# Attention in a one-core transformer block: the next head's high and low parts made in thirds on ScalarE and VectorE instead of whole on ScalarE and GpSimd

## The reference, cut to what matters

```python
def block_attention(q, k, v):          # q, k: 96 wide; v: 64 wide; 8 heads
    scale = dk ** -0.5
    qb = q.reshape(B, nb, Q_BLOCK, H, dk).transpose(1, 0, 2, 3, 4)
    def one_block(qblk):
        s = jnp.einsum('bqhd,bkhd->bhqk', qblk, k).astype(jnp.float32) * scale
        p = jax.nn.softmax(s, axis=-1).astype(v.dtype)
        return jnp.einsum('bhqk,bkhd->bqhd', p, v)
```

## Time and profile before

| what | value |
|---|---|
| three runs | 3381.17, 3385.09, 3386.98 us; median 3385.09 |
| the profiled execution's own time | 3376.51 us |
| its span, first to last instruction | 3374.7 us |
| mean granted TensorE clock | 0.944 |
| TensorE busy | 3056.5 us, 91% of the span |
| VectorE busy | 1946.7 us, 58% |
| ScalarE busy | 1373.7 us, 41% |
| GpSimd busy | 648.9 us, 19% |

### The profile page before, as it was taken

One profiled execution on the slowest core, in us unless ns is written; L12 is line 12 of the kernel. 1 busy time (PEld: TensorE's weight loads), 2 busy tenths in 40 slices (PEclk: granted clock), 3 DMA queues, 4 the chain that ended last, 5 costly groups with the idle time before them and its releaser, 6 DMA issues. The chain is left out here.

```text
span 3374.7 us, 43955 instructions
## 1 busy us (share of the span) xinstructions
PE 3056.5 (91%) x14693; PEld 2172.2 (64%) x14693; DVE 1946.7 (58%) x2632; ACT 1373.7 (41%) x2061; POOL 648.9 (19%) x459
## 2 busy tenths in 40 slices
PE   6799999999887699999999999799399999999992
PEld 1355555555587455655665565687399899989992
DVE  1133333333476578777777776445767666767663
ACT  0133333333222556656665665211244444444442
POOL 0011111111254233232233222221001010101011
PEclk9899999999877899999999999899599999999996
DMA  8512111111221201101110100433467576767666
GB/s 318 155 63 69 64 62 62 65 66 57 86 95 55 50 4 32 33 7 29 33 26 10 32 5 5 171 131 112 139 203 219 184 221 201 220 189 224 201 179 237
DMA packets 254709, 363.74 MB, mean 108 GB/s; under 512 B 36436, under 2 KB 170583, under 8 KB 252888
## 3 DMA queue, kind: packets, MB, share of 16 engines
q1 hardware_dynamic: 245336, 327.97, 30.4%
q0 software_dynamic: 9216, 33.56, 4.4%
HBM read 279.65 MB, written 81.83 MB: 107 GB/s over the span
## 5 line engine op out<-in xcount | busy, mean ns | idle before, releaser
L467 PE MATMUL bank<-w_in_sb,h_T 128*128 128x512 f32 (+1 forms) x1440 | 609.3, 578 | 2.1 <-DVE h_T L616 2.1
L1648 PE MATMUL ebank<-gathered_T,w_gate_up 128*128 128x256 f32 x4608 | 561.6, 284 | 22.8 <-issue 13.8
L1648 PEld LDWEIGHTS ebank<-gathered_T,w_gate_up 128*128 128x128 f32 x4608 | 557.3, 191 | 26.5 <-issue 17.6
L1077 PE MATMUL abank<-scores,head_v 128*128 128x512 f32 x1152 | 547.1, 603 | 2.2 <-ACT scores L1115 2.2
L1040 PE MATMUL abank<-head_qT,head_kT 96*128 96x512 f32 x1728 | 505.4, 437 | 24.2 <-POOL head_qT L1019 24.2
L467 PEld LDWEIGHTS bank<-w_in_sb,h_T 128*128 128x128 f32 x1440 | 270.1, 191 | 299.0 <-issue 298.8
L1040 PEld LDWEIGHTS abank<-head_qT,head_kT 96*128 96x128 f32 x1728 | 327.9, 190 | 171.9 <-issue 95.8
L1103 ACT ACTIVATE scores<-abank 128x512 f32<-128x512 f32 x576 | 314.5, 608 | 77.5 <-PE abank L1040 71.7
L1077 PEld LDWEIGHTS abank<-scores,head_v 128*128 128x128 f32 x1152 | 218.4, 194 | 181.4 <-issue 163.8
L1026 POOL TENSOR_TENSOR scores<-scores,max_for_pool 128x1536 f32<-128x1536 f32 x64 | 221.0, 3474 | 571.9 <-ACT max_for_pool L1109 571.9
L1115 ACT ACTIVATE scores<-scores 128x1536 f32<-128x1536 f32 x192 | 287.4, 1498 | 40.0 <-DVE scores L1157 35.6
(11 more groups left out here) (258 smaller groups left out, 3465.2 us busy)
## 6 DMA issues: line engine op xcount, KB each, us to landing
w_gate_up_whole<-in_w_exp_gate SPq DMA_DIRECT2D x48, 1024.0 KB, 5.6
w_gate_up_whole<-in_w_exp_up SPq DMA_DIRECT2D x48, 1024.0 KB, 9.0
w_down_whole<-in_w_exp_down SPq DMA_DIRECT2D x192, 256.0 KB, 4.8
ada_w<-in_w_ada SPq DMA_DIRECT2D x12, 2048.0 KB, 12.6
scratch_ret<-ret_rows SPq DMA_DIRECT2D x72, 256.0 KB, 2.6
x_tile<-in_x_all SPq DMA_DIRECT2D x18, 512.0 KB
w_in_sb<-in_w_in SPq DMA_DIRECT2D x4, 2048.0 KB, 19.0
chunk_qk<-scratch_ret SPq DMA_DIRECT2D x16, 512.0 KB
```

Source lines behind the costliest of these rows:

```text
L467: m = pe.matmul(banks[bank][:, 0:n], hT[u][:, k, :], w_in[:, k, lo:lo + n], start=(k == 0), stop=(k == KD - 1))
L1077: m = pe.matmul(banks[5 + j % 2][:, :], v1[u][:, kt, :], sc[j % 2][:, kt, :], start=(kt == 0), stop=(kt == T - 1))
L1648: x = pe.matmul(banks[f % 3][:, j * CAP:(j + 1) * CAP], w_gu[c][:, wp, j, k, o:o + P], xsT[:, xp, k, :], start=(k == 0 and n == 0), stop=( ...
```

## The change

- A turn's split is now a third of the columns (768; of the queries 768, 768 and 512). Turns `j` 0, 1, 2 split the odd head of the pair, turns 4, 5, 6 the even head of the next.
- ScalarE makes the rounded copies of the third where it made the whole ones, behind the last copy of scores and ahead of the copy of the maxima.
- The subtractions move from GpSimd to VectorE, and stand behind the shift of groups 0 and 1 and ahead of the output.
- The first head's split is in thirds on ScalarE and VectorE too.
- Keys and queries count into one semaphore per parity, values into another. ScalarE waits for keys and queries alone. TensorE waits for the first head's values and for the ones column only behind the first block's scores.
- `modulation`'s semaphores are cleared and freed behind its block, and an empty block (a barrier) follows.

```diff
@@ -116,6 +116,21 @@
     return parts, whole
 
 
+@contextmanager
+def stage_semaphores(nc):
+
+    taken = []
+
+    def sem(name):
+        taken.append(nc.alloc_semaphore(name=name))
+        return taken[-1]
+
+    yield sem
+    nc.clear_and_free_semaphores(taken)
+    with nc.Block():
+        pass
+
+
 def mid(ap, n):
 
     p, a = ap.shape
@@ -144,12 +159,9 @@
 
 def modulation(nc, ins, perm, scratch, weights, w_loaded):
 
-    with ExitStack() as ctx:
+    with stage_semaphores(nc) as sem, ExitStack() as ctx:
         def sb(name, shape, dt=F32):
             return ctx.enter_context(nc.sbuf_tensor(name, shape, dt))
-
-        def sem(name):
-            return ctx.enter_context(nc.semaphore(name))
 
         NCH = 12
         CW = 6 * D // NCH
@@ -964,7 +976,7 @@
         o_sb = sb("out_T", [64, QB])
         ms = sb("max_for_pool", [P, QB])
         banks = [ctx.enter_context(nc.psum_tensor(f"abank{b}", [P, 512], F32)) for b in range(8)]
-        kv_loaded = ParitySignal(nc, ctx, "head_kv_loaded", 4)
+        kq_loaded, v_loaded = ParitySignal(nc, ctx, "head_kq_loaded", 3), ParitySignal(nc, ctx, "head_v_loaded")
         ones_set = ctx.enter_context(nc.semaphore("ones_set"))
         assert nc.sbuf_base <= perm["mix_at"], (nc.sbuf_base, perm["mix_at"])
         block = ctx.enter_context(nc.Block())
@@ -977,21 +989,28 @@
             for j in range(2 * NB):
                 turn(H // 2 - 1, j, BLOCKS - 2 * NB + j, j < 2 * NB - 1)
 
+        THIRD = TOK // 3
+
+        def thirds(u, n):
+
+            c = slice(n * THIRD, (n + 1) * THIRD)
+            return (kT[u], k_whole[u], c), (qT[u], q_whole[u], slice(c.start, min(c.stop, SEQ)))
+
         def split_next(split, pair, j):
 
-            if j == 1:
-                split(pair * 2 + 1, 1)
-            if j == 5 and not (isinstance(pair, int) and pair == H // 2 - 1):
-                split(pair * 2 + 2, 0)
+            if j < 3:
+                split(pair * 2 + 1, 1, j)
+            if 4 <= j < 7 and not (isinstance(pair, int) and pair == H // 2 - 1):
+                split(pair * 2 + 2, 0, j - 4)
 
         @block.sync
         def _(sp):
             def load(head, u):
-                for dst, src in ((k_whole[u][0:NOPE, 1, :], scratch["kT_heads"][bass.ds(head, 1), :, :].rearrange("o d n -> (o d) n")),
-                                 (k_whole[u][NOPE:DQ, 1, :], scratch["krT"]),
-                                 (q_whole[u][:, 1, :], scratch["qT"][bass.ds(head, 1), :, CTX:].rearrange("o d n -> (o d) n")),
-                                 (v1[u][:, :, 0:DV], scratch["v"].rearrange("(t p) (h d) -> p t h d", p=P, h=H)[:, :, bass.ds(head, 1), :].rearrange("p t o d -> p t (o d)"))):
-                    sp.dma_start(dst, src).then_inc(kv_loaded.sems[u], 32)
+                for dst, src, loaded in ((k_whole[u][0:NOPE, 1, :], scratch["kT_heads"][bass.ds(head, 1), :, :].rearrange("o d n -> (o d) n"), kq_loaded),
+                                 (k_whole[u][NOPE:DQ, 1, :], scratch["krT"], kq_loaded),
+                                 (q_whole[u][:, 1, :], scratch["qT"][bass.ds(head, 1), :, CTX:].rearrange("o d n -> (o d) n"), kq_loaded),
+                                 (v1[u][:, :, 0:DV], scratch["v"].rearrange("(t p) (h d) -> p t h d", p=P, h=H)[:, :, bass.ds(head, 1), :].rearrange("p t o d -> p t (o d)"), v_loaded)):
+                    sp.dma_start(dst, src).then_inc(loaded.sems[u], 32)
 
             load(0, 0)
             load(1, 1)
@@ -1011,22 +1030,13 @@
             for u in range(2):
                 pool.memset(v1[u][:, :, DV:], 1.0).then_inc(ones_set, 1)
 
-            def split(head, u, parts=(0, 1)):
-
-                for n in parts:
-                    x, whole = ((kT[u], k_whole[u]), (qT[u], q_whole[u]))[n]
-                    sg["rounded"].wait(pool, head, n + 1)
-                    pool.tensor_tensor(x[:, 1, :], whole[:, 1, :], x[:, 0, :].bitcast(F32), ALU.subtract).then_inc(sg["rest"].sem, 1)
-
             def turn(pair, j, b, more):
                 s = sc[j % 2]
                 for g in range(4, GROUPS):
                     x = s[:, g * G:(g + 1) * G, :]
                     sg["max_copied"].wait(pool, b)
                     pool.tensor_tensor(x, x, mid(ms[:, :], G), ALU.subtract).then_inc(sg["shifted_pool"].sem, 1)
-                split_next(split, pair, j)
-
-            split(0, 0, parts=(1,))
+
             loop(pool, turn)
 
         @block.tensor
@@ -1041,7 +1051,8 @@
                 m.then_inc(sg["s_psum"].sem, 1)
 
             def head_ready(head, u):
-                kv_loaded.wait(pe, head, u)
+                kq_loaded.wait(pe, head, u)
+                v_loaded.wait(pe, head, u)
                 sg["rounded"].wait(pe, head)
                 sg["rest"].wait(pe, head)
 
@@ -1081,21 +1092,23 @@
                         max_spread(b + 1)
                 m.then_inc(sg["out_psum"].sem, 1)
 
-            pe.wait_ge(ones_set, 2)
-            head_ready(0, 0)
+            sg["rounded"].wait(pe, 0)
+            sg["rest"].wait(pe, 0)
             for kt in range(T):
                 score(0, 0, 0, kt)
             max_rows(0)
             max_spread(0)
+            pe.wait_ge(ones_set, 2)
+            v_loaded.wait(pe, 0, 0)
             loop(pe, turn)
 
         @block.scalar
         def _(act):
-            def split(head, u):
-
-                kv_loaded.wait(act, head, u)
-                for x, whole in ((kT[u], k_whole[u]), (qT[u], q_whole[u])):
-                    act.activation(x[:, 0, :], whole[:, 1, :], ACT.Copy).then_inc(sg["rounded"].sem, 1)
+            def split(head, u, n):
+
+                kq_loaded.wait(act, head, u)
+                for x, whole, c in thirds(u, n):
+                    act.activation(x[:, 0, c], whole[:, 1, c], ACT.Copy).then_inc(sg["rounded"].sem, 1)
 
             def copy_scores(j, b, g):
                 for kt in range(g * G, (g + 1) * G):
@@ -1121,7 +1134,8 @@
                 if more:
                     copy_max(b + 1)
 
-            split(0, 0)
+            for n in range(3):
+                split(0, 0, n)
             for g in range(GROUPS):
                 copy_scores(0, 0, g)
             copy_max(0)
@@ -1129,6 +1143,12 @@
 
         @block.vector
         def _(dve):
+            def split(head, u, n):
+
+                for i, (x, whole, c) in enumerate(thirds(u, n)):
+                    sg["rounded"].wait(dve, head, 2 * n + i + 1)
+                    dve.tensor_tensor(x[:, 1, c], whole[:, 1, c], x[:, 0, c].bitcast(F32), ALU.subtract).then_inc(sg["rest"].sem, 1)
+
             def maximum(j, b, g):
 
                 s = sc[j % 2]
@@ -1173,10 +1193,11 @@
                     spread(b + 1)
                     for g in (0, 1):
                         shift((j + 1) % 2, b + 1, g)
+                split_next(split, pair, j)
                 output(j, b)
 
-            sg["rounded"].wait(dve, 0, 1)
-            dve.tensor_tensor(kT[0][:, 1, :], k_whole[0][:, 1, :], kT[0][:, 0, :].bitcast(F32), ALU.subtract).then_inc(sg["rest"].sem, 1)
+            for n in range(3):
+                split(0, 0, n)
             for g in range(1, GROUPS):
                 maximum(0, 0, g)
             spread(0)
@@ -1185,7 +1206,7 @@
             loop(dve, turn)
 
 
-ATTENTION_STEPS = {"rounded": 2, "rest": 2, "s_psum": 18, "scores": 18, "max_keys": 7, "max_T": 1, "max_rep": 2,
+ATTENTION_STEPS = {"rounded": 6, "rest": 6, "s_psum": 18, "scores": 18, "max_keys": 7, "max_T": 1, "max_rep": 2,
                    "max_psum": 2, "shifted": 4, "shifted_pool": 2, "max_copied": 1, "probs": 6, "out_psum": 1, "out": 2, "out_stored": 1}
 ATTENTION_DMAS = ("out_stored",)
```

More of the change, by code:

```diff
@@ L3 @@
 from concourse import mybir
-from contextlib import ExitStack
+from contextlib import ExitStack, contextmanager
 F32 = mybir.dt.float32
```

## The result

The changed kernel takes 3467.43 us (median of four runs, 3464.28 to 3473.10), the kernel before 3385.51 in the same comparison. The ratio is 1.0246, with a 95% interval of 1.0228 to 1.0264: 82 us slower, where 3461 us was forecast.

What follows compares the result with a forecast made beforehand. TensorE was taken to bound attention's loop (busy 904 of 935 us); -45.3 + 126 - 6 + 1.5 = +76 us on the profiled 3376.5 gives 3453, or 3461 us for the median. Range 3402 to 3493 us.

Steps and rivals of the forecast that it cites:

- What goes: Attention's loop: GpSimd's subtractions leave seven turns, and with them TensorE's waits for the last maxima.
- Term 1: Attention's loop: the extra length of seven turns with a split goes, -45.3 us.
- Term 2: Attention's loop: VectorE's subtractions meet GpSimd's shifts; TensorE loses 4.1 us plus 1.9 for clock in 21 turns, +126 us.
- The clock: Attention's loop: TensorE's clock falls to 0.50 behind each new wait, costing 1.9 us each.
- rival 1: Attention's loop: the waits come but TensorE's clock doesn't fall, +36 us, 3421 us; chance 0.13.
- ScalarE and the load: Attention's loop: two copies of 0.8 us in 21 turns fit ScalarE's 8.2 us wait; earlier loads have landed: nothing.
- Terms 3 and 4: Attention's start gets shorter, -6 us; clearing semaphores at the border of two stages costs +1.5 us.
- Rival 4: Attention's loop: the new wait takes just what the old gave, 3385 us; chance 0.03.
- rival 2: Attention's loop: both thirds go in between GpSimd's two shifts, TensorE loses 1.3 us a turn, 3362 us; chance 0.07.
- Rival 3: Attention's loop: subtractions and GpSimd's shifts don't meet, 0.2 us a turn, -46 us, 3339 us; chance 0.09.
- The sum: Whole kernel: -45.3 + 126 - 6 + 1.5 = +76 us on the profiled 3376.5 us; median forecast 3461 us.

Runs made afterwards that it cites:

- seventh experiment: Changed kernel with only each head's last third subtracted behind the spread of the maxima, ahead of the shifts: 3421.87 us, ratio 1.0116 to the kernel before.
- fifth experiment: Changed kernel with the loop's splits as before, whole and subtracted on GpSimd, leaving the new start and semaphores: 3377.69 us, ratio 0.9983 to the kernel before.
- the sixth: Kernel before with only the modulation's 19 semaphores cleared and the empty block behind it: 3385.65 us, ratio 1.0006.
- eighth experiment: Changed kernel with the loop's splits whole in turns 1 and 5, VectorE subtracting ahead of the shifts: 3341.12 us, ratio 0.9877 to the kernel before.
- the first: Changed kernel with VectorE's subtractions moved behind the spread of the maxima, ahead of the shifts: 3334.85 us, ratio 0.9861 to the kernel before.
- the second experiment: Changed kernel with GpSimd's shift of groups 4 and 5 cut to one column of 512: 3339.80 us, ratio 0.9881 to the kernel before.
- third experiment: Changed kernel with the loop's splits whole in turns 1 and 5, VectorE subtracting ahead of the output: 3396.65 us, ratio 1.0044 to the kernel before.

## Why the prediction was right, point by point

- **What goes.** Right. The seven waits and VectorE's long L1147 and L1151 are gone (0.69 and 0.43 us at their means). Term 1 stands at -45.3 us. The prediction's rule on what waits, an instruction that reads both its inputs from SBUF, leaves out one kind. Before the change a copy with a single input in SBUF took 3.17 us in place of 0.43, ending 0.3 us behind GpSimd's subtraction for the queries (1319.40 + 4.95 us in the earlier trace rows):

```profile
1321.46 3.17 DVE L1151 COPY score_max<-max_cols 128x512 f32<-128x512 f32 x1
```

- **Term 2, the meetings.** Right in its mechanism and nearly in size. Keys 2.04 us (2.0), queries 4.25 (3.9), reciprocal 4.8 us late (4.5), the tenth tile 4.47 us late (4.1). The step that was off is GpSimd's second shift: held up by 0.73 us, not 0.5; and the slack ahead of the tile was 0.3 us, not 0.4. Term 2 measured 139 us where 126 was forecast, and the missing 13 lie in the lateness: 100 us where the sum had 21 x 4.1 = 86.
- **The head change was missed.** The prediction sent all 21 turns by ScalarE's copies. Seven go straight from the last subtraction to TensorE: the turn behind it begins with the new head's scores, 5.3 us late. The seventh experiment shows it as a cost of its own. The size came out near because the same late subtraction makes both waits, 5.3 us in place of 4.47, so that the miss is worth some 6 us in all. That is luck: it would have misled anyone who moved the subtractions behind the output.
- **The clock.** Right in kind: 0.50 for some microseconds around each wait, and so rival 1 falls. Right in size too: 1.9 us for each of 21 waits, as taken. The three waits of a head differ, though: 2.6, 1.3 and 1.7 us. Counted against the profile's idle time (88 us in 21 waits) the clock would seem to cost 51 us, 2.4 each, but 12 of these are the 0.56 us by which each wait is longer than its idle time.
- **ScalarE and the load.** Right: its copies took 0.83 us each and no turn waits for them or for the load.
- **Terms 3 and 4.** -6.7 us (-6) and +0.5 (+1.5). The fifth experiment's start saved 7.5 us in its profile, the sixth's border grew by 0.5. No row had shown what clearing semaphores costs, and the 1.5 was a choice.
- **The rivals.** Rival 4 falls with the 82 us. The order in which the two engines went in, which rival 2 reversed, was retention's: one by one. The Trainium skill's rule in "SBUF — State Buffer", section "SBUF: two separate sides", by which the first to start holds the ports for its whole instruction, agrees with 2.04 and 4.25 us here and with GpSimd's 8.52 us in the eighth experiment. Rival 3, no meeting, is what the first and the second experiment had to be built for, and its 3339 us are near what they took (3335 and 3340).
- **The sum.** Made against the profiled execution, it was +76 us; that pair of profiles gives +92.3. Of the 16 missing, about 12 are the size of term 2 (92.8 + 45.3 = 138 by the accounts, against 126) and 5.6 the retention, and the start and the semaphores take 1.6 off. Between the medians the difference is 82 us. That 3461 lies only 6 us from 3467 owes something to chance: the profile of before lay 8.6 us under its median, that of after 1.4 us above.

## What to carry to other kernels

Before work is moved to VectorE, look at what GpSimd does in that very stretch: an instruction with both inputs in SBUF cost there not its own time alone but also the rest of GpSimd's instruction, once for each, so that cutting it in pieces multiplied the price. VectorE's shifts, with one input from PSUM, kept their 1.7 us beside GpSimd's. Look for a gap in which VectorE waits for an engine other than GpSimd and GpSimd is idle; here 1.9 us of work fitted into 1.86 us of waiting, and the same change became 1.4% faster in place of 2.5% slower. And give each moved piece its deadline: who needs it first, and in which turn.

## What the runs showed of the hardware that was not expected

- Both engines can be the one that waits. GpSimd's pair of shifts took 6.90 us alone, 7.63 against thirds, 9.22 against whole subtractions and 8.52 where VectorE was first, while VectorE's own instructions in that last case took 2.55 and 2.28 us, as alone.
- The clock fell at different points of like waits. Both waits amid scores are 3.91 us: in the first it was at 0.50 before the scores went on at 1318.53 us, and stayed there until 1324; in the second it was still at 1.00 when they went on at 1354.79, and was back at 1.00 by 1359. That is how one cost 2.6 us and the other 1.3. At the head change it fell within the wait of 4.76 us (0.65 and 0.50 in its third and fourth microsecond) and stayed until 4 us behind it.
- The border from retention to attention lay between 1093.7 us (before) and 1107.2 us (third experiment) in ten profiles, though the code ahead of it differs at most by the semaphores' 0.5 us. Single profiles of this kernel can't settle 6 us.
